# Two norms split by token stream, a dense half computed stream by stream, and a gather placed directly behind the ranks

## The chip, the core and the metric

The kernel runs on one core of a Trainium2 chip. The metric is the time of one execution on the device in microseconds (us). Below, TensorE (PE) is the matrix engine, VectorE (DVE) and ScalarE (ACT) are the two elementwise engines, GpSimd (POOL) a slower one, and SyncE (SP) issues most of the DMAs.

## What is computed

Two layers of a diffusion backbone over 256 latent and 256 context tokens (two streams, two tiles of 128 tokens each) of width 1024, all in float32:

```python
for l in range(DEPTH):                       # DEPTH = 2
    h  = _modulate(x, norm1_w[l], sh1, sc1)  # rms norm * (1 + scale) + shift
    hc = _modulate(ctx, norm1_w[l], csh1, csc1)
    p, pc = h @ w_in[l], hc @ w_in[l]        # last layer: only the key/value columns of pc
    ...                                      # attention, retention, convolution
    x = x + g1 * (concat(att, ret, cnv) @ w_out[l])
    h2 = _modulate(x, norm2_w[l], sh2, sc2)
    x = x + g2 * _channel_mixer(h2, l, ...)
    # the context goes the same way in layer 0 and ends there

def _swiglu(h, wg, wu, wd):                  # layer 0, D_FF = 2816
    return (silu(h @ wg) * (h @ wu)) @ wd

def _moe(h, router, wg, wu, wd):             # layer 1, 8 experts, D_FF_EXPERT = 3584
    top_v, top_i = lax.top_k(h @ router, 2)
    combine = sum(one_hot(top_i) * softmax(top_v)[..., None])
    return sum(combine[..., e:e+1] * _swiglu(h, wg[e], wu[e], wd[e]) for e in range(8))
```

## The kernel before

**Products.** Weights and activations are split into a high part (float32r, written by ScalarE) and a low part (the rest, a subtraction on VectorE). `three` (L517) issues three products for each pair of operands: high x high, high x low, low x high. Weights come as items of up to 1 MB: SyncE loads one into one of four `raw` slots when the item that held the slot has its low part (to L1076), ScalarE writes the high part into a `parts` slot that TensorE has finished with (`split_to`, L1126; `split_expert`, L1234), VectorE the low part (L1457, L1841). The order is fixed for each engine by the program text; semaphores (`after`, `wait_ge`) join them.

**Norms.** ScalarE squares each token tile with a sum (`squares`), GpSimd takes the root (`root_squares`), VectorE scales (`scale_tokens`), TensorE transposes the scaled tiles into banks (`turn_normalized`, L558), VectorE modulates the latent banks and ScalarE the context ones (`modulate`), ScalarE writes high parts into `hTr`, VectorE low parts. In front of the dense layer and of layer 1 this runs for all four tiles together, after the residual of the last of them.

**Order around the change.** Output projection of layer 0 (`project_out`, two halves of 512 columns, tiles in the order 2, 3, 0, 1, where 2 and 3 are the context), second norm, dense layer (`dense_ffn`: 11 tiles of gate and up, two halves of the down product, and once more), first norm of layer 1 for both streams, in-projection of layer 1 (`project_in`, first the query columns, for which only the latent tiles are needed), attention and the rest, output projection, second norm of the latent tiles, `routing`, `place_tokens`, `scatter_matrices`, `spread_gate`, then `experts`. The experts run in four pairs (`pair`, a loop for the last three); each expert has seven slices of gate, up and down. Tokens of an expert are gathered with a product (`gather`, matrix `PA` of zeros and ones), and its output goes back with a product per token tile and half (`scatter`, matrix `SCAT`, in full float32) and an addition into `ACC`. The matrix of the scatter carries the combine weights; it is made by `weighted` on VectorE, turned by `scatter_matrices` on TensorE and kept in `SA`.

**Banks.** VectorE evacuates four banks in turn (`open_v`), ScalarE three (`open_a`). TensorE waits in `open_v` or `open_a` until the bank's last user is read.

## Time and profile before

| | before |
|---|---|
| runs, us | 2016.98, 2017.33, 2013.34; median 2016.98 |
| profiled execution, us | 2017.29, its span 2015.3 |
| busy, share of the span | PE 92%, weight loads 74%, DVE 67%, ACT 51%, POOL 6% |
| chain that ended last | PE 78%, DVE 11%, DMA 5%, ACT 3%, issue 2%, POOL 1% |
| DMA | 472.89 MB, mean 235 GB/s |
| first product of the dense layer | 369.49 us |
| first product of layer 1 | 771.86 us |
| first product of the experts | 994.66 us |

A timeline row gives start, duration, engine, source line, operation, and in brackets how long the engine had been idle and who released it. Where rows of one kind are merged, "x32" counts them and the duration covers them all. Busy time is no measure of how well TensorE is used, since the ends of its products are modelled and overlap; its idle times are.

### The profile page before, as it was taken

The page shows a single profiled execution, that of the slowest core. Times are in us where ns is not written, and L with a number is a line of the kernel's source. Part 1 is how long each engine was busy: PE and PEld are TensorE (multiplying, and loading weights), DVE is VectorE, ACT ScalarE, POOL GpSimd, SP SyncE. Part 2 cuts the span into 40 slices and gives each one's busy share as a digit, 9 for nine tenths or more (in the row PEclk, how much of TensorE's full clock was granted, in tenths as well). Part 3 has the DMA queues.
Part 4 walks back from the last instruction along what each step waited for, and adds up shares of the span by engine and source line. Part 5 has one row for each costly group of instructions (what it writes and reads, how often), then busy time and mean ns, then how long its engine had stood idle before and what let it go on. Part 6 is the DMA issues. An engine that isn't in the chain of part 4 may idle for free.

```text
span 2015.3 us, 23614 instructions
## 1 busy us (share of the span) xinstructions
PE 1857.1 (92%) x8916; PEld 1499.9 (74%) x8916; DVE 1350.3 (67%) x1286; ACT 1036.7 (51%) x972; POOL 115.4 (6%) x127
## 2 busy tenths in 40 slices
PE   4899888799999987998699999999999999999997
PEld 1777457688788767857588888788887888878885
DVE  1464964432243225685698988989888888888886
ACT  2322542432122115263377776777767767667773
POOL 0021710100000000250000000000000000000000
PEclk9899989899999998998799999999999999999999
DMA  8223832432333112392499998999999999899994
GB/s 291 84 88 125 302 133 71 106 88 90 84 105 100 58 58 89 105 334 84 145 370 334 374 366 313 358 336 373 357 328 354 346 357 373 328 350 339 366 367 157
DMA packets 245914, 472.89 MB, mean 235 GB/s; under 512 B 10546, under 2 KB 60564, under 8 KB 245804
## 3 DMA queue, kind: packets, MB, share of 16 engines
q1 hardware_dynamic: 241856, 468.67, 65.5%
q10 hardware_dynamic: 3948, 2.67, 0.5%
q8 instruction: 79, 1.29, 0.3%
q14 instruction: 31, 0.25, 0.0%
HBM read 470.26 MB, written 1.05 MB: 234 GB/s over the span
## 4 chain that ended last, share of the span: by engine, by line
PE 78%; DVE 11%; DMA 5%; ACT 3%; issue 2%; POOL 1%; SPq 0%; ACTq 0%; DVEq 0%; POOLq 0%
PE bank L519 23%; PE bank L521 22%; PE bank L520 22%; DVE parts L1479 2%; DVE parts L1464 2%; PE bank L537 1%; PE bank L920 1%; DMA raw<-in_ada_w_dram 1%; PE bank L934 1%; ACT parts L1240 1%; PE bank L961 1%; DMA raw<-in_moe_w_gate_dram 1%; DMA raw<-in_moe_w_up_dram 1%; PE bank L753 1%; ACT parts L1138 1%
## 5 line engine op out<-in xcount | busy, mean ns | idle before, releaser
L1479 DVE TENSOR_TENSOR parts<-raw,parts 128x2048 fp32r<-128x2048 f32 x336 | 765.0, 2289 | 113.1 <-ACT parts L1240 112.0
L1240 ACT ACTIVATE parts<-raw 128x2048 fp32r<-128x2048 f32 x336 | 642.4, 1918 | 259.6 <-DMA raw<-in_moe_w_up_dram 90.1
L519 PE MATMUL bank<-parts,XEr 128*128 128x512 f32 x896 | 355.0, 396 | 7.7 <-DVE XEr L1479 3.9
L521 PE MATMUL bank<-parts,XEr 128*128 128x512 f32 x896 | 350.0, 391 | 0.0
L520 PE MATMUL bank<-parts,XEr 128*128 128x512 f32 x896 | 349.6, 390 | 0.0
L1138 ACT ACTIVATE parts<-raw 128x2048 fp32r<-128x2048 f32 (+1 forms) x62 | 113.3, 1831 | 331.1 <-PE bank L521 308.4
L1464 DVE TENSOR_TENSOR parts<-raw,parts 128x2048 fp32r<-128x2048 f32 (+1 forms) x62 | 135.4, 2188 | 194.1 <-ACT parts L1138 194.0
L519 PEld LDWEIGHTS bank<-parts,XEr 128*128 128x128 f32 x896 | 168.6, 188 | 43.4 <-DVE parts L1479 5.9
L521 PEld LDWEIGHTS bank<-parts,XEr 128*128 128x128 f32 x896 | 168.6, 188 | 35.8
L520 PEld LDWEIGHTS bank<-parts,XEr 128*128 128x128 f32 x896 | 168.8, 188 | 33.5
L519 PE MATMUL bank<-parts,HTr 128*128 128x512 f32 x448 | 180.8, 404 | 0.7 <-DVE parts L1479 0.7
L521 PE MATMUL bank<-parts,HTr 128*128 128x512 f32 x448 | 174.6, 390 | 0.0
L520 PE MATMUL bank<-parts,HTr 128*128 128x512 f32 x448 | 174.4, 389 | 0.0
L519 PE MATMUL bank<-hTr,parts 128*128 128x512 f32 (+1 forms) x416 | 160.7, 386 | 5.3 <-DVE parts L1464 2.1
L521 PE MATMUL bank<-hTr,parts 128*128 128x512 f32 (+1 forms) x416 | 158.6, 381 | 0.0
L520 PE MATMUL bank<-hTr,parts 128*128 128x512 f32 (+1 forms) x416 | 158.6, 381 | 0.0
L519 PE MATMUL bank<-parts,hTr 128*128 128x512 f32 (+1 forms) x320 | 124.3, 389 | 18.5 <-DVE hTr L1479 8.6
L521 PE MATMUL bank<-parts,hTr 128*128 128x512 f32 (+1 forms) x320 | 122.4, 382 | 0.0
L520 PE MATMUL bank<-parts,hTr 128*128 128x512 f32 (+1 forms) x320 | 122.2, 382 | 0.0
L1479 DVE TENSOR_TENSOR HF<-bank,SG 128x512 f32<-128x512 f32 x22 | 15.2, 692 | 145.4 <-PE bank L521 145.4
L519 PEld LDWEIGHTS bank<-parts,HTr 128*128 128x128 f32 x448 | 84.1, 188 | 22.0 <-issue 3.3
L520 PEld LDWEIGHTS bank<-parts,HTr 128*128 128x128 f32 x448 | 84.2, 188 | 20.3 <-issue 3.3
(220 smaller groups left out, 2319.0 us busy)
## 6 DMA issues: line engine op xcount, KB each, us to landing
raw<-in_moe_w_gate_dram SPq DMA_DIRECT2D x112, 1024.0 KB, 7.0
raw<-in_moe_w_up_dram SPq DMA_DIRECT2D x112, 1024.0 KB, 7.2
raw<-in_moe_w_down_dram SPq DMA_DIRECT2D x112, 1024.0 KB, 6.6
raw<-in_ada_w_dram SPq DMA_DIRECT2D x28, 1024.0 KB, 7.8
more<-in_ada_w_dram SPq DMA_DIRECT2D x20, 1024.0 KB, 7.5
raw<-in_w_in_dram SPq DMA_DIRECT2D x12, 1024.0 KB, 5.4
raw<-in_ffn_w_gate_dram SPq DMA_DIRECT2D x22, 512.0 KB, 4.0
raw<-in_ffn_w_up_dram SPq DMA_DIRECT2D x22, 512.0 KB, 5.3
```

What stands on the lines that cost most here:

```text
L519: nc.tensor.matmul(out, st[0], mv[0], start=start, stop=False)
L520: nc.tensor.matmul(out, st[0], mv[1], start=False, stop=False)
L521: return nc.tensor.matmul(out, st[1], mv[0], start=False, stop=stop)
L537: mm = nc.tensor.matmul(b[32 * j:32 * j + 32, :], cond[:, half * KT // 2 + j, c0:c0 + 32], w[:, j, :], start=opening, stop=closing)
L753: mm = nc.tensor.matmul(OB[:, head * 64:(head + 1) * 64], PT[:, n % 4, kb * P:(kb + 1) * P], proj[:, kb, C_V + 64 * g:C_V + 64 * g + 64], ...
L920: mm = nc.tensor.matmul(M[k // 4][:, (k % 4) * P:(k % 4 + 1) * P], xn[:, t, k * P:(k + 1) * P], PA[:, t, bass.ds(i * 2 + j, 1), :].rearran ...
L934: nc.tensor.matmul(M[h][:, :], SCAT[:, ee % 2, t * P:(t + 1) * P], YS[:, h * 512:(h + 1) * 512], start=True, stop=True).then_inc(scatter_f ...
L961: mm = nc.tensor.transpose(T[g % 2][:, j * P:(j + 1) * P], HE[:, g % 2, j * P:(j + 1) * P], ident)
L1138: nc.scalar.activation(parts[:, s, 0, 0:k * width], raw[:, r, 0:k * width], ACT.Copy).then_inc(hi_ready, 1)
L1240: nc.scalar.activation(parts[:, n % PARTS, 0, :], raw[:, r, :], ACT.Copy).then_inc(hi_ready, 1)
L1464: nc.vector.tensor_tensor(parts[:, s, 1, 0:k * width], raw[:, r, 0:k * width], parts_f[:, s, 0, 0:k * width], ALU.subtract).then_inc(lo_re ...
L1479: return nc.vector.tensor_tensor(out, a, b, op)
```

## The change

1. *Second norm of layer 0.* The context tiles are scaled, transposed, modulated and split first (`modulate_second(1)`), while the last latent tile still gets its residual; then the latent tiles. TensorE's first feed-forward tile (`first_hidden`) is computed per stream, 256 columns at a time, with the latent transposes between the context's gate and up products.
2. *Last half of the last dense down product.* It runs first for the latent tiles over all three items, which stay in their slots, then for the context tiles. The latent norm of layer 1 (`squares(early=True)`, `scale_tokens(early=True)`, `modulate_first`, `first_low`) runs beside the context half, its transposes (`turn_stream(0)`) go ahead of that half's last item. The context norm of layer 1 comes inside the first column slice (`turn_stream(1)`, `modulate_context`). The decay factors move behind it.
3. *Routing.* The matrix `PA` is written directly behind the ranks, and the first gather needs only it. The scatter matrices are the transposed `PA` (`turn_places`, in the first slice of the first pair); the combine weight is multiplied in when the scattered rows are added (`share`). One of four splits and the clearing of `ACC` leave VectorE's way; the spreading of the gate moves into the output projection of layer 1.
4. *Scatter.* The expert's output is split into a high and a low part (`YS`), `SCAT` is float32r, and each product of the scatter becomes two. The gathered tokens' high and low parts are written in halves.

```diff
             def dense_ffn():
+                first_hidden()
 ...
+            def turn_second(s, banks):
+                after(xn_ready, TT)
+                for kp, b in enumerate(banks):
+                    for kk in range(2):
+                        for t in range(TT):
+                            k = 2 * kp + kk
+                            mm = nc.tensor.transpose(b[:, (kk * TT + t) * P:(kk * TT + t + 1) * P],
+                                                     xn[:, s * TT + t, k * P:(k + 1) * P], ident)
+                    mm.then_inc(a_full if kp % 2 else v_full, 1)
+            def first_hidden():
+                turn_second(1, open_second(1))
+                n, hi, lo = next_item()
+                x_banks = open_second(0)
+                outs = [open_a(("gate", 0)), open_v(("up", 0))]
+                for s in (1, 0):
+                    c = slice(s * SEQ, (s + 1) * SEQ)
+                    for half, b in enumerate(outs):
+                        for k in range(KT):
+                            if half == 0 and k % (KT // 2) == 0:
+                                after(h_lo, KT // 4)
+                            mm = three(b[:, c], (hi[:, k, half * P:(half + 1) * P], lo[:, k, half * P:(half + 1) * P]),
+                                       (hTr[:, 0, k, c], hTr[:, 1, k, c]), k == 0, k == KT - 1)
+                        if s == 0:
+                            mm.then_inc(v_full if half else a_full, 1)
+                        elif half == 0:
+                            turn_second(0, x_banks)
 ...
-                    for half in range(2):
+                    for half in range(2 if p0 == 0 else 1):
 ...
+                held = []
+                for s in range(2):
+                    outs = [open_v() for _ in range(TT)]
+                    for j, (f0, f1) in enumerate(ff_split):
+                        if s == 0:
+                            held.append(next_item())
+                        n, hi, lo = held[j]
+                        if s and f1 == HALF_FF:
+                            turn_stream(0)
+                        for f in range(f0, f1):
+                            for t in range(TT):
+                                tok = slice((s * TT + t) * P, (s * TT + t + 1) * P)
+                                mm = three(outs[t][:, :], (HFr[:, 0, f, tok], HFr[:, 1, f, tok]),
+                                           (hi[:, f - f0, :], lo[:, f - f0, :]), f == 0, f == HALF_FF - 1)
 ...                                                       # project_in
-                            after(h_lo, KT // 2)
+                            after(h_lo, KT // 4 if layer else KT // 2)
+                            if layer and t == 1 and a == C_Q and k0:
+                                turn_stream(1)
 ...                                                       # project_out
+                    if layer and half == 0:
+                        spread_gate(5, (0,))
 ...                                                       # TensorE, experts
-                        nc.tensor.matmul(M[h][:, :], SCAT[:, ee % 2, t * P:(t + 1) * P], YS[:, h * 512:(h + 1) * 512],
-                                         start=True, stop=True).then_inc(scatter_full, 1)
+                        for part_ in range(2):
+                            mm = nc.tensor.matmul(M[h][:, :], SCAT[:, ee % 2, t * P:(t + 1) * P],
+                                                  YS[:, part_, h * 512:(h + 1) * 512], start=part_ == 0, stop=part_ == 1)
+                        mm.then_inc(scatter_full, 1)
+                def turn_places():
+                    pe.wait_ge(places, 2 * part + 2)
+                    for q in range(PAIRS):
+                        if q >= 2:
+                            pe.wait_ge(places_read, PAIRS * part + q - 1)
+                        ...                               # four transposes of PA into T[q % 2]
+                        mm.then_inc(places_full, 1)
 ...                                                       # SyncE
                 if n == first["ffn"] + 2:
-                    sp.wait_ge(v_full, job[("mixed", 0)])
+                    sp.wait_ge(act_mix, 1)
 ...                                                       # ScalarE
+                def expert_high(i, ee):
+                    act.wait_ge(down_done, i * PAIR_SLICES + (s0 + EF_SLICES * (ee + 1) + CREDIT))
+                    for h in range(2):
+                        nc.scalar.activation(YS[:, 0, h * 512:(h + 1) * 512], Y[h][:, :], ACT.Copy).then_inc(y_high, 1)
 ...
                 squares(order_of(layer))
                 if layer == 0:
+                    modulate_second(1)
+                    modulate_second(0)
+                    split_to(O + 7)
                     small_loads(1)
-                    modulate(1)
 ...
+                    squares(range(TT), early=True)
+                    split_to(first["in", 1] + 1)
+                    after(mod1_ready)
+                    modulate_first()
+                    split_to(first["in", 1] + 2)
 ...                                                       # VectorE
+                if layer == 0:
+                    for t in (2, 3, 0):
+                        add_gated(1, t, True)
+                    scale_tokens((2, 3))
+                    add_gated(1, 1, True)
+                    modulate_second(1)
+                    dve.wait_ge(x_ready, x_count[0])
+                    scale_tokens((0, 1))
+                    modulate_second(0)
+                    split_to(O + 7)
 ...
+                    scale_tokens(range(TT), early=True)
+                    split_to(first["in", 1] + 1)
+                    first_low()
+                    for t in range(TT, NT):
+                        add_gated(1, t, True)
 ...                                                       # next layer, then the second item's low part
-                scale_tokens(range(NT))
+                scale_tokens(range(TT if layer else 0, NT))
 ...
-            for n in range(PARTS):
+            for n in range(PARTS - 1):
                 split_expert(0, n, 0)
             route()
             place_tokens(0)
-            nc.vector.memset(ACC_t[:, :], 0.0).then_inc(scatter_read, 1)
+            split_expert(0, PARTS - 1, 0)
 ...
-                        tt(acc, M[h][:, :], acc, ALU.add).then_inc(scatter_read, 1)
+                        nc.vector.scalar_tensor_tensor(acc, M[h][:, :], share[:, ee % 2, t:t + 1], acc, ALU.mult, ALU.add)\
+                            .then_inc(scatter_read, 1)
```

## Rows read from the trace of the kernel before

**Rows 1.** The page's first part: busy time of each engine.
```profile
PE 1857.1 (92%) x8916; PEld 1499.9 (74%) x8916; DVE 1350.3 (67%) x1286; ACT 1036.7 (51%) x972; POOL 115.4 (6%) x127
```

**Rows 2.** Timeline of TensorE in front of the dense layer: start, duration, operation.
```profile
362.18 6.17 PE L568 MATMUL bank<-const,xn 128*128 128x128 f32 x32 [15.79 <-DVE xn L1512]
369.49 0.47 PE L519 MATMUL bank<-hTr,parts 128*128 128x512 f32 x1 [1.14 <-DVE hTr L1479]
```

**Rows 3.** Timelines of VectorE and ScalarE in the second norm of layer 0.
```profile
343.71 0.69 DVE L1479 TENSOR_TENSOR YG<-bank,gb 128x512 f32<-128x512 f32 x1 [1.21 <-PE bank L521]
346.43 0.69 DVE L1479 TENSOR_TENSOR YG<-bank,gb 128x512 f32<-128x512 f32 x1 [1.30 <-PE bank L521]
...
357.22 0.75 DVE L1512 TENSOR_SCALAR xn<-X,rstd 128x1024 f32<-128x1024 f32 x1 [0.80 <-POOL rstd L1403]
...
365.04 1.00 DVE L1526 TENSOR_SCALAR hTf<-bank,scl,ada 128x256 f32<-128x256 f32 x2 [0.71 <-PE bank L568]
365.95 1.28 DVE L1479 TENSOR_TENSOR hTr<-hTf,hTr 128x512 fp32r<-128x512 f32 x2
...
354.01 1.04 ACT L1161 ACTIVATE xn<-X 128x1024 f32<-128x1024 f32 x1
...
354.95 0.19 ACT L1161 ACTIVATION_READ_ACCUMULATOR xn<-X 128x1 f32 x1
...
366.14 1.02 ACT L1169 ACTIVATE hTf<-bank,ada,scl 128x256 f32<-128x256 f32 x2
367.04 1.16 ACT L1175 ACTIVATE hTr<-hTf 128x512 fp32r<-128x512 f32 x2
```

**Rows 4.** Timeline of TensorE: last dense half, norm of layer 1, second column slice.
```profile
718.76 0.70 PE L519 MATMUL bank<-parts,HFr 128*128 128x512 f32 x1 [2.93 <-DVE YG L1479]
...
764.54 6.37 PE L568 MATMUL bank<-const,xn 128*128 128x128 f32 x32 [13.98 <-DVE xn L1512]
...
785.58 0.41 PE L519 MATMUL bank<-parts,hTr 128*128 128x384 f32 x1 [2.56 <-DVE parts L1464]
```

**Rows 5.** Busy time by stretch: length, PE, PEld, DVE, ACT, POOL, PEclk, DMA share, GB/s.
```profile
788.00:790.00 2.00, 2.00 (x8) 2.00 (x8) 0.00 (x0) 0.00 (x0) 0.00 (x0) 0.50 1.01 330
```

**Rows 6.** Timelines of TensorE, VectorE and ScalarE between layer 1's projection and the experts.
```profile
954.29 3.63 PE L568 MATMUL bank<-const,xn 128*128 128x128 f32 x16 [4.41 <-DVE xn L1512]
...
986.99 3.81 PE L920 MATMUL bank<-PA,xn 128*128 128x128 f32 x32 [1.38 <-DVE ACC L2004]
994.66 0.50 PE L519 MATMUL bank<-parts,XEr 128*128 128x512 f32 x1 [3.87 <-DVE XEr L1479]
...
959.04 8.89 DVE L1479 TENSOR_TENSOR parts<-raw,parts 128x2048 fp32r<-128x2048 f32 x4
...
974.08 1.95 DVE L1823 TENSOR_SCALAR XF<-const,top 128x128 f32<-128x128 f32 x8
...
992.29 1.06 ACT L1254 ACTIVATE XEr<-XF 128x1024 fp32r<-128x1024 f32 x1 [1.74 <-DVE XF L1853]
```

**Rows 7.** Timeline of TensorE: products of 256 columns following one another.
```profile
837.66 0.28 PE L520 MATMUL bank<-hTr,parts 128*128 128x256 f32 x1
837.78 0.28 PE L521 MATMUL bank<-hTr,parts 128*128 128x256 f32 x1
```

**Rows 8.** Expert stage: a scatter in the chain, two stretches, groups, one load.
```profile
1139.97 1.72 PE bank L934 x4
...
1240.00:1260.00 20.00, 18.73 (x82) 15.00 (x81) 18.06 (x12) 14.66 (x9) 0.00 (x0) 1.00 0.77 281
1640.00:1720.00 80.00, 80.00 (x355) 64.85 (x354) 71.86 (x44) 57.71 (x39) 0.00 (x0) 1.00 1.01 366
...
L1240 ACT ACTIVATE parts<-raw 128x2048 fp32r<-128x2048 f32 x336 | 642.4, 1918 | 259.6 <-DMA raw<-in_moe_w_up_dram 90.1
...
L1542 DVE SCALAR_TENSOR_TENSOR decay<-distance,dneg,decay 128x512 f32<-128x512 f32 x8 | 5.5, 747 | 0.1
...
raw<-in_moe_w_gate_dram SPq DMA_DIRECT2D x112, 1024.0 KB, 7.0
```

291 lines of the change are left out of this document (206 added, 85 removed).

## The prediction

> **What bounds the kernel now.** I read the page first (shares of the span, busy tenths), then TensorE's waits, then each engine's timeline in the three places that the change touches, and last the busy time by stretch of the expert stage. TensorE is busy for 92% of the span [rows 1]: nearly all of what can be won is pauses of TensorE, and there are few. The reader should see three. Between the output projection of layer 0 and the dense layer it waits 15.8 us for the normalized tokens, then transposes for 6.2 us at half clock, and the first product stands at 369.49 [rows 2]; the last one before the pause had ended at 362.18 - 15.79 = 346.4. Between the dense layer and layer 1 it waits 2.9 us for a bank ahead of the last half [rows 4], 14.0 us for the normalized tokens [rows 4] and, after the first column slice, 2.6 us for split weights [rows 4]. Before the experts it works in scraps between 954.29 - 4.41 = 949.9 and 994.66, 45 us, while VectorE ranks tokens and writes matrices [rows 6]. After such pauses come stretches in which the granted clock is 0.50, the 1.2 GHz level: after the wait that ended at 785.58 it stood at 0.50 at 788 to 790 [rows 5]. In the expert stage TensorE has no pause to speak of except at the pair boundaries, where 20 us hold 18.7 us of work and the loads drop to 281 GB/s [rows 8]. So the stage goes by TensorE, with the loads right behind it.
>
> **Second norm of layer 0.** Work on TensorE stays the same: 32 transposes and 48 products of 512 columns, now 96 of 256. A 256-column product follows the last one after 0.12 us [rows 7], a 512-column one after 2.72 / 12 = 0.227 us (one token tile's 12 products separate the two multiplies at 343.71 and 346.43) [rows 3], so halving the width costs 96 x 0.12 - 48 x 0.227, some 0.6 us. The order is 2, 3, 0, 1, so the context tiles 2 and 3 are full at 338.3 and 341.0, and their residual is added by 342.5. ScalarE squares tile 2 from 341.2 and tile 3 until 343.7 (1.04 + 0.19 each), and from the end of a square to the scaled tile it is 357.22 - 355.14 = 2.1 us [rows 3]: context scaled at 347.4. TensorE pauses 1.0 us and transposes. ScalarE squares tile 1 first (until 350.1: its residual comes after the scaling), then takes 1.02 us for a bank and 0.58 for a high part, VectorE 0.99 and 0.64 [rows 3]: four high parts are out at 354.5, the low parts of the first half at 353.1. TensorE starts the gate product of the context at 353.4, needs 2.8 us for it, waits until 356.7 for the latent tiles, transposes them (3.1 us at half clock), and does the remaining three quarter-items in 8.5 us: first feed-forward tile done at 368.3. Before, that tile ends at 369.49 + 0.5 + 10.9 = 380.9. **-12.5 us** (-9 to -15: the hops of semaphores are in the rows, but a pause of 2.8 us in the middle can bring a half-clock stretch of 1.9 us). Its cover: the latent norm lies under the up product of the context; were that gone, 5 us would return. Of the queues: the load of the third feed-forward item now waits for the last SiLU of the mixing instead of the end of the projection; it goes out earlier, and nothing behind it on the queue is due sooner. The small loads of ScalarE's queue come behind the norm instead of in front of it.
>
> **Last dense half by streams, joined to layer 1.** The half opened four banks, so it waited for all four evacuations, 2.9 us, and its first nine products ran at half clock (0.43 us apart, 1.8 us lost) [rows 4]. By streams it opens two, free 2.7 us sooner: start at 716.1, and I take the half-clock stretch as gone too. Latent tiles are then full at 716.1 + 66 x 0.227 = 731.1, and 15 us of context products lie over their residual (2.7), squares, scaling (to 736.8). The transposes come after two of the three items at 742.0, about 2.1 us at full clock, and the down product ends at 748.2. ScalarE modulates beside it (four times 1.02 + 0.58 and a hop, until 749.2), so the first slice starts at 748.2 without a wait, first half to 753.6. The second item's slot frees at 748.2: its high part is out at 751.1, but on VectorE the low part is queued behind the context's residual (752.6), squares (753.8) and scaling (755.6): ready at 757.9. That is the wait that the change adds, 4.3 us, behind it the whole in-projection. Then 2.7 + 2.1 (context transposes) + 2.7 us: the slice of 384 columns begins at 765.2. With 1 us for hops and clock, 766; before it is 785.58 [rows 4]. **-19.5 us** (-14 to -22). Next late is the context's low part, due at 769.3, ready at about 768: an even race, up to 2 us.
>
> **Ranks and first gather.** Removed ahead of the first gather: one of four splits (8.89 / 4 = 2.2 us), the memset, the weighted matrices, their transposes and copies; the first write of a matrix stands at 974.08, the gather at 986.99 [rows 6]. The gate's spreading (16 products, by the gather's row 16 x 0.12 = 1.9 us) moves into the output projection of layer 1, where TensorE is full: +1.9 us. So: the first write at 974.08 - 0.2 (a small memset in front of it) - 2.2 + 1.9 + 0.2 (room for a hop) = 973.8; the first expert's two writes at 0.24 us each (1.95 / 8) [rows 6], gather from 974.4. TensorE stood idle before, so I take half clock, 7.0 us where the row has 3.81: 981.5. VectorE is through its 16 writes and the split at 980.3; last half of the gathered tokens 1.4 us, low part of the first half 0.7: experts start at 983.8 instead of 994.66, -10.9 us. But 16 transposes come into the first pair. They are some 2 us of TensorE; the third of them waits for ScalarE's copy of the first, and that is queued behind a split of 1.92 us [rows 8]: 3.8 us. **-7 us** (-3 to -10).
>
> **Scatter.** Before, one tile of one expert is four full-precision records in 1.72 us [rows 8]; after, four products of the width and type of the gate products, 4 x 0.227 = 0.91 us. 16 such, two of them in the tail, where ScalarE's copy ahead of VectorE's subtraction takes half back: 14 x 0.81 + 0.7 = 12 us. Of it the six at the start of pairs two to four fall where the supply has just dropped [rows 8], and I count half: **-9.5 us** (-3 to -13). On VectorE the copy becomes a subtraction of the same length; the add becomes an operation with a scalar, 747 ns where the nearest row has it [rows 8] against 0.69, +2 us in 1000, under TensorE's work. ScalarE gets 1.2 us more per expert. **Gathered high part in halves**: a half (0.53 of 1.06 us [rows 6]) goes ahead of the wait for VectorE, three boundaries: **-1 us** (0 to -1.5).
>
> A rule against this term: the rows show 366 GB/s over 80 us with DMA share 1.01 [rows 8]. The Trainium skill, SBUF — State Buffer, section A bandwidth-pool intuition that's wrong, gives about 358 GB/s between HBM and one core and calls HBM nearly always the end-to-end bottleneck. The trace does not agree with the figure: measured stretches pass it. By it the 352 MB of expert weights take at least 984 us (an estimate from that page), the scatter would still gain, but with little room left; by the trace's rate the room is larger.
>
> The memset of the accumulator goes to GpSimd beside VectorE's splits. The same page, section SBUF: two separate sides, says that the two engines share a port pair under an exclusive lock, but a VectorE operation with two SBUF inputs only against a GpSimd one that reads SBUF. A memset reads nothing, so by this rule it is free; no row here shows the pair together.
>
> **Sum.** -12.5 - 19.5 - 7 - 9.5 - 1 = -49.5 us against the profiled execution's own 2017.3 (span 2015.3 and 2.0 around it), which is 0.3 above the median of the runs: 1967.8, say **1968 us**.
>
> **Rivals.**
> *The supply takes over in the expert stage.* For it: share of DMA at 1.0 and 366 GB/s in the full stretches; where TensorE has only products it asks for 1.05 MB per 2.8 us, 374 GB/s. Against: per pair TensorE has extra work of gathers and scatters worth over 10 us that the loads don't need, and the boundary costs them about 20 x (1 - 281/366) = 4.6. Then -9.5 and -1 go: 1978.5. Chance 0.15.
> *New short pauses bring half clock.* Each of three joints (after the context's transposes, after the first slice's half, after the gather) costs 1.9 us more and the last dense half keeps its own 1.8: 1975.5. For it: rows 5 after a wait of 2.6 us. Against: after 16 us of pause the feed-forward started with 0.227 us products, since transposes went before. 0.15.
> *The joint doesn't join.* In-order queues put the other stream's work ahead, so that both norms end as late as before: only -7, -9.5 and -1 stay: 2000. Against: the orders above, worked through engine by engine. 0.05.
> *The added wait on ScalarE starves the ring; slower than before.* ScalarE now waits for an expert's last down product in front of its next splits. If at every of the eight expert ends the four raw slots drain, one load of 7.0 us [rows 8] is lost each: 8 x 7 = 56, so 2024. It decides from 49.5 / 8 = 6.2 us per expert end. Against: in the middle of a pair the split in front of the wait has waited for the same down product already, to free its slot; at the pair boundary VectorE waits for it now in the same place. 0.03.
>
> **How the numbers follow.** Forecast 0.62. Ends of the five terms together give 1956 and 1988; not all fall to one side, so 1956 to 1984, which takes in the first two rivals and leaves out the last two and a tail. About 0.2% is what a measurement of this kernel can tell from no change, 4 us: faster 0.95, same 0.02, slower 0.03.
>
> **What would show it.** TensorE's wait for xn in front of the transposes: 1 us in the first joint, none in the second; the last dense half starting under 1 us after the half before; a wait for split weights of 4 us in the first slice of layer 1; experts starting 43 us (12.5 + 19.5 + 10.9) earlier than now, at about 952; a scatter of 0.91 us; from there to the end about 7 us less than the 1020 of now. Wrong it would be with waits of TensorE for parts in each pair (supply), clock 0.50 in stretches that now have 1.00, or a wait for xn over 5 us.

## The result: 2.7% faster, and where the 54 us lie

The changed kernel takes 1961.78 us (median of four executions, 1959.30 to 1965.86) against 2017.15 of the kernel before: a ratio of 0.9731 with a 95% interval of 0.9711 to 0.9751. The forecast was 1968 within 1956 to 1984. The profiled execution of the changed kernel took 1963.41 us, with a span of 1961.6.

The page of the changed kernel, first part and chain of work that ended last:

```profile
PE 1836.7 (94%) x8964; PEld 1494.4 (76%) x8964; DVE 1346.2 (69%) x1282; ACT 1048.7 (53%) x1001; POOL 113.6 (6%) x126
...
PE 63%; DVE 15%; DMA 12%; ACT 5%; issue 4%; POOL 0%; SPq 0%; DVEq 0%; ACTq 0%; POOLq 0%
```

Of the 53.7 us between the spans, 20 are busy time of TensorE (rows 1 against this page) and 33 its pauses. The last chain has changed: before, it was 78% TensorE and 5% DMA; now it runs over transfers and splits for longer stretches. That comes back in the experiments.

Four moments cut the span into sections that can be compared between all kernels, whatever happened ahead of them: the end of the output projection of layer 0 (start of its last product plus 0.39), VectorE's first write of HF (the first feed-forward tile is through), the first product of 384 columns in layer 1, and the first product of the experts. All from the timelines, in us:

| kernel | projection 0 ends | first HF | 384 columns | experts | span | to HF | to 384 | to experts | stage |
|---|---|---|---|---|---|---|---|---|---|
| before | 346.39 | 381.45 | 785.58 | 994.66 | 2015.3 | 35.06 | 404.13 | 209.08 | 1020.6 |
| after | 344.75 | 366.46 | 752.59 | 947.21 | 1961.6 | 21.71 | 386.13 | 194.62 | 1014.4 |
| difference | -1.64 | | | | -53.7 | -13.35 | -18.00 | -14.46 | -6.2 |

**First joint.** The changed TensorE in front of the dense layer, then VectorE and GpSimd in the same stretch:

```profile
344.96 1.94 PE L882 MATMUL bank<-const,xn 128*128 128x128 f32 x16 [0.21 <-DVE xn L1672]
350.60 0.36 PE L530 MATMUL bank<-hTr,parts 128*128 128x256 f32 x1 [3.70 <-ACT hTf L1291]
...
354.65 0.41 PE L532 MATMUL bank<-hTr,parts 128*128 128x256 f32 x1
354.87 2.17 PE L882 MATMUL bank<-const,xn 128*128 128x128 f32 x16
```

```profile
343.40 1.41 DVE L1672 TENSOR_SCALAR xn<-X,rstd 128x1024 f32<-128x1024 f32 x2
344.79 0.69 DVE L1638 TENSOR_TENSOR YG<-bank,gb 128x512 f32<-128x512 f32 x1
...
342.13 0.19 POOL L1554 TENSOR_SCALAR lnt<-ssq 128x2 f32<-128x2 f32 x1 [61.90 <-ACT xn L1244]
342.47 0.70 POOL L1555 TENSOR_TENSOR rstd<-lnt,nhalf 128x2 f32<-128x2 f32 x1
```

Where 15.79 us of waiting stood [rows 2], there are now 0.21 and 3.70. Both context tiles are scaled before the last tile's residual, and the latent transposes at 354.87 wait for nothing. The products of 256 columns just ahead of them follow one another after 0.21 us where full clock has 0.12: behind the wait of 3.70, from 352.0 to 354.8, the granted clock was 0.50, the 1.2 GHz level.

**Second joint.** TensorE from the last dense half on, and the busy time of two stretches:

```profile
700.48 0.47 PE L530 MATMUL bank<-parts,HFr 128*128 128x512 f32 x1
...
726.44 1.47 PE L598 MATMUL bank<-const,xnx 128*128 128x128 f32 x12
...
732.81 0.39 PE L530 MATMUL bank<-parts,hTr 128*128 128x512 f32 x1
...
742.95 0.80 PE L530 MATMUL bank<-parts,hTr 128*128 128x512 f32 x1 [4.54 <-DVE parts L1623]
...
748.10 1.91 PE L598 MATMUL bank<-const,xn 128*128 128x128 f32 x16
...
752.59 0.33 PE L530 MATMUL bank<-parts,hTr 128*128 128x384 f32 x1
```

```profile
742.95:747.95 5.00, 5.00 (x12) 0.50 0.76 230
...
700.00:735.00 35.00, 34.58 (x160) 1.00 0.25 83
```

The waits of 2.93 and 13.98 us [rows 4] are gone, and the first slice starts at 732.81 without one. In their place stands one wait of 4.54 for the split weights, and behind it twelve products at a granted clock of 0.50.

**Third joint.** VectorE, GpSimd and TensorE ahead of the experts:

```profile
931.60 1.80 POOL L1605 MEMSET ACC<- 128x2048 f32 x1 [12.88 <-PE bank L966]
...
931.99 0.17 DVE L1638 TENSOR_TENSOR top<-top,best 128x16 f32<-128x16 f32 x1
932.19 1.24 DVE L1995 TENSOR_SCALAR top<-top 128x16 f32<-128x16 f32 x1
...
934.71 0.17 DVE L1995 TENSOR_SCALAR top<-top 128x16 f32<-128x16 f32 x1
...
938.59 4.18 DVE L2027 TENSOR_SCALAR PA<-const,top 128x128 f32<-128x128 f32 x16
...
939.44 5.26 PE L991 MATMUL bank<-PA,xn 128*128 128x128 f32 x32 [1.31 <-DVE PA L2027]
947.21 0.47 PE L530 MATMUL bank<-parts,XEr 128*128 128x512 f32 x1 [2.51 <-DVE XEr L1638]
```

The gather follows VectorE's first write after 0.85 us; before, 12.9 us lay between them [rows 6]. The odd row is L1995: one operation of 16 columns takes 1.24 us, its twin 2.5 us later 0.17.

**Expert stage.** The scatter in the chain and its group:

```profile
1112.35 0.93 PE bank L1006 x4
```

```profile
L1006 PE MATMUL bank<-YS,SCAT 128*128 128x512 f32 x64 | 19.2, 424 | 2.1 <-DVE YS L1638 2.1
```

Four records in 0.93 us where they took 1.72 [rows 8].

### The profile page after: what moved, and what is told of

Its sections match the earlier page's. It is cut to its first block, busy times and chain, and to the rows that moved or that the text cites. A ratio compares the mean times of both kernels' runs of the same rounds, so it can differ in the third digit from the quotient of the medians.

```text
span 1961.6 us, 23758 instructions
## 1 busy us (share of the span) xinstructions
PE 1836.7 (94%) x8964; PEld 1494.4 (76%) x8964; DVE 1346.2 (69%) x1282; ACT 1048.7 (53%) x1001; POOL 113.6 (6%) x126
## 4 chain that ended last, share of the span: by engine, by line
PE 63%; DVE 15%; DMA 12%; ACT 5%; issue 4%; POOL 0%; SPq 0%; DVEq 0%; ACTq 0%; POOLq 0%
PE bank L530 18%; PE bank L532 18%; PE bank L531 18%; DVE parts L1638 5%; DMA raw<-in_moe_w_gate_dram 5%; ACT parts L1358 3%; DMA raw<-in_moe_w_up_dram 3%; DMA raw<-in_moe_w_down_dram 3%; DMA raw<-in_ada_w_dram 2%; DVE parts L1623 2%; PE bank L548 1%; PE bank L991 1%; DVE gb L1897 1%; PE bank L781 1%; PE bank L1046 1%
## 5 line engine op out<-in xcount | busy, mean ns | idle before, releaser
L530 PE MATMUL bank<-parts,HTr 128*128 128x512 f32 x448 | 175.3, 391 | 1.1 <-DVE HTr L1638 0.7
L531 PE MATMUL bank<-parts,HTr 128*128 128x512 f32 x448 | 174.5, 390 | 0.0
L532 PE MATMUL bank<-parts,HTr 128*128 128x512 f32 x448 | 174.4, 389 | 0.0
L530 PE MATMUL bank<-hTr,parts 128*128 128x512 f32 (+1 forms) x432 | 164.6, 381 | 7.3 <-ACT hTf L1291 3.7
L532 PE MATMUL bank<-hTr,parts 128*128 128x512 f32 (+1 forms) x432 | 162.5, 376 | 0.0
L531 PE MATMUL bank<-hTr,parts 128*128 128x512 f32 (+1 forms) x432 | 162.4, 376 | 0.0
L530 PEld LDWEIGHTS bank<-hTr,parts 128*128 128x128 f32 x432 | 82.2, 190 | 24.0 <-issue 7.2
L530 PEld LDWEIGHTS bank<-parts,HTr 128*128 128x128 f32 x448 | 84.1, 188 | 20.5 <-DVE parts L1638 2.3
```

The costliest lines, as they stand in the source:

```text
L530: nc.tensor.matmul(out, st[0], mv[0], start=start, stop=False)
L531: nc.tensor.matmul(out, st[0], mv[1], start=False, stop=False)
L532: return nc.tensor.matmul(out, st[1], mv[0], start=False, stop=stop)
```

## The experiments

Each ran beside the kernel before; "beside it" is a kernel on the same chip in the same series (e_same with the next three, e_norm2_old to e_four_banks, e_same_2 with the last three). The middle series has no unedited kernel in it, so its medians are compared with unedited kernels of other series, and its sections count for more. The sections of all of them, in us, read as in the table above:

| kernel | median | ratio to before, 95% | to HF | to 384 | to experts | stage |
|---|---|---|---|---|---|---|
| e_same | 1964.88 | 0.9722-0.9753 | 21.72 | 386.14 | 194.69 | 1024.1 |
| e_scatter_fp32 | 1973.49 | 0.9759-0.9795 | 21.69 | 386.13 | 194.66 | 1022.3 |
| e_scatter_one | 1963.89 | 0.9720-0.9754 | 21.69 | 386.13 | 194.68 | 1012.2 |
| e_memset_twice | 1966.26 | 0.9722-0.9762 | 21.73 | 386.16 | 196.12 | 1013.9 |
| e_norm2_old | 1975.93 | 0.9784-0.9824 | 31.55 | 386.66 | 193.61 | 1018.3 |
| e_dense_old | 1981.73 | 0.9820-0.9859 | 21.71 | 403.70 | 194.27 | 1013.8 |
| e_split_early | 1958.39 | 0.9701-0.9739 | 21.71 | 381.96 | 194.23 | 1017.4 |
| e_four_banks | 1963.31 | 0.9727-0.9762 | 21.71 | 386.13 | 196.03 | 1015.5 |
| e_same_2 | 1964.15 | 0.9742-0.9782 | 21.72 | 386.18 | 194.63 | 1014.5 |
| e_less_bytes | 1957.25 | 0.9707-0.9746 | 21.72 | 386.18 | 194.66 | 1008.0 |
| e_less_bytes_one | 1953.44 | 0.9681-0.9718 | 21.73 | 386.16 | 194.63 | 1003.7 |
| e_combined | 1958.87 | 0.9712-0.9747 | 21.71 | 381.97 | 194.45 | 1015.0 |

The table can be read before any single run. The columns "to HF" and "to 384" repeat to 0.05 us wherever their code is the same, so a change of 1 us there is certain. One value seems to break this: "to 384" is 386.66 in e_norm2_old, with the code of the changed kernel from HF on. The moment "first HF" is VectorE's: in the changed kernel it comes 0.8 us after TensorE has finished that tile (365.68), because VectorE still splits weights, and in e_norm2_old 0.03 us after it. So "to HF" shows some 0.5 us less than the new order gains, and "to 384" as much more; the same explains the last 0.4 us between 404.13 and e_dense_old's 403.70.

The stage doesn't repeat: the unedited kernel gave 1014.4, 1024.1 and 1014.5. In that stage one pair of profiles proves nothing under 10 us, and the medians have to speak. They too are blunt: the five executions of one kernel spread over 4 to 9 us, and a difference of two means of five is known to about 3 to 5 us (95% interval).

### The unedited kernel again

> The changed kernel itself, unedited, as the yardstick for the kernels beside it. Both theories: within 0.2% of 1961.8 us. Of the 53.7 us between the two spans, 1.6 us lie before the first edited instruction (the output projection of layer 0 ended at 344.75 us of its execution in the changed kernel's profile against 346.39 before). If they are a matter of the one execution (how long the granted clock stays at half in the first 345 us), the end of that projection lies here somewhere between 344.5 and 346.5; if something in the changed code brings them, it is 344.7 again.

The projection of layer 0 ended at 343.84, and at 347.27 in the highest of the twelve further executions, all with the same code up to there. The 1.6 us ahead of the change are a matter of the execution.

The profiled execution is also the slowest of its five (1972.40), by the stage alone: 1024.1. TensorE's waits in it, whole tail of the kernel, then those of the first profile of the same code:

```profile
PE bank L530 <- DVE parts L1638: 8.3, 15, 0.9
...
PE bank L530 <- DVE HTr L1638: 1.2, 4, 0.5
```

```profile
PE bank L530 <- DVE parts L1638: 4.3, 8, 0.9
...
PE bank L530 <- DVE HTr L1638: 0.7, 1, 0.7
```

Weights came late fifteen times instead of eight. The chain of that execution is 50% TensorE and 19% DMA, against 63 and 12. The same program asks for the same bytes; in the third quarter of the stage they came at 348 GB/s in this execution and at 356 in the first.

### Is the expert stage still TensorE's?

Full-precision scatter, and a scatter with half its products:

```
-                        for part_ in range(2):
-                            mm = nc.tensor.matmul(M[h][:, :], SCAT[:, ee % 2, t * P:(t + 1) * P],
-                                                  YS[:, part_, h * 512:(h + 1) * 512], start=part_ == 0, stop=part_ == 1)
+                        mm = nc.tensor.matmul(M[h][:, :], SCAT[:, ee % 2, t * P:(t + 1) * P],
+                                              YS[:, 0, h * 512:(h + 1) * 512], start=True, stop=True)
```

For the first of them YS and SCAT are F32 as well, so one full-precision product does what two did. The second leaves the low part of the expert outputs out.

> Expert outputs and scatter matrices as float32 and one full-precision product per half instead of two float32r products; ScalarE's copy and VectorE's subtraction stay, so only TensorE changes: 16 tile-experts at 1.72 instead of 0.91 us, +13 us of TensorE. The output keeps full precision. TensorE sets the pace of the expert stage: +9.5 to +13 us (1971 to 1975). The supply of weights sets it: the added work lies in waits for parts, which shrink by as much, under +3 us.

Measured +8.6 us beside e_same (1973.49 - 1964.88), for some 13 us of TensorE; by the means it is 6.4, give or take 4.7 (95%, here and below). The chain is 80% TensorE and 4% DMA again.

> Only the product with the high part of the expert outputs is left in each scatter (the low part is still formed but not multiplied, so the output lacks it): 16 x 0.45 = 7.3 us less on TensorE. TensorE sets the pace: -6 to -7 us (1955). The supply sets it by now: TensorE waits for parts for those 7 us, 0 to -1 us. Between them, with the six scatters at the pair starts lost and the rest won: -4 us.

Measured -1.0 us (1963.89 - 1964.88; by the means -2.0, give or take 4.6), for 7.3 us of TensorE. Two stretches of 50 us of this kernel (length, PE, PEld, DVE, ACT, POOL, PEclk, DMA share, GB/s) show TensorE busy for 47 and 48 of 50 us and the DMA queues almost full; its waits for weights are these:

```profile
1198.52:1248.52 50.00, 47.20 (x209) 37.75 (x208) 45.02 (x31) 35.88 (x25) 0.00 (x0) 1.00 0.96 336
1848.52:1898.52 50.00, 48.19 (x215) 39.23 (x216) 43.72 (x26) 35.81 (x24) 0.00 (x0) 1.00 0.99 352
```

```profile
PE bank L530 <- DVE parts L1637: 6.5, 8, 1.1
```

They are 2.2 us more than in two unedited profiles (4.3 and 4.2) and less than in the third (8.3), so they do not show where the 7.3 us went. By the medians, a microsecond of TensorE costs about 0.66 us above the changed kernel and 0.14 below it; given the spread, that bend is suggested and not shown. If it is there, the supply of weights would explain it, and the next two runs test that by taking bytes away instead of work: they load only 768 of the 1024 columns of each down weight, and the last quarter holds old data, so the result is another.

```
-                            dst = raw[:, n % RAW, :].rearrange("p (k n) -> p k n", k=2)
+                            dst = raw[:, n % RAW, :].rearrange("p (k n) -> p k n", k=2)[:, :, 0:768]
+                            rows = rows[:, :, 0:768]
```

> The loads of the experts' down weights fetch 768 of 1024 columns, 8% fewer bytes in the expert stage, with everything else unchanged (the last quarter of those columns is stale, so the output is another). The supply sets the pace at the margin, as the run with one scatter product suggested: the waits for weights (4 to 8 us) go and the stage becomes as long as TensorE's own work, -5 to -10 us, 1954 to 1958, and its length varies less from execution to execution. TensorE sets the pace and the run with one product had some other loss: -1 to -2 us.

Measured -6.9 us beside e_same_2 (1957.25 - 1964.15), though no instruction of TensorE, ScalarE or VectorE changed. By the means it is 7.2, give or take 3.8: clear of the spread, and the one run that shows the supply costing time in the changed kernel. The stage took 1008.0, the DMA rate fell to 316 GB/s over 1000 us from 346, and the waits for weights from 4.2 to 2.6:

```profile
947.55:1947.55 1000.00, 989.13 (x4592) 819.84 (x4592) 867.61 (x558) 719.54 (x513) 0.00 (x0) 1.00 0.90 316
```

```profile
PE 83%; DVE 9%; DMA 3%; ACT 3%; issue 2%; POOL 0%; SPq 0%; ACTq 0%; DVEq 0%; POOLq 0%
```

> Both at once: 768 of 1024 columns of the down weights are loaded, and only the high part of the expert outputs is multiplied in the scatter (both change the output). If the supply hid the 7.3 us of TensorE's work that the single product saves, they appear now: 7 us less than with fewer bytes alone. If they stay hidden (under 2 us less), something other than the supply holds the stage, such as VectorE's own chain at the scatters.

Measured -3.8 us beside e_less_bytes (by the means -5.1, give or take 3.4). So TensorE's time counts as well when there are fewer bytes. Whether it counts for more than with all bytes, which is what "the supply hid it" claims, these runs don't decide: -1.0 and -3.8 lie within each other's spread. They point that way, no more. The expected 7 did not come; the chain still has 7% DMA, and TensorE waits for weights for 4.1 us, so the supply may not be quite out of the way. Fewer bytes still weren't tried.

> The changed kernel unedited once more, beside the three others on the same chip: their yardstick. Within 0.2% of 1963 us; its expert stage, from the first product to the end, 1014 to 1024 us long (the two profiled executions so far gave 1014.4 and 1024.1, with 4.3 and 8.3 us of waits for weights).

Measured 1964.15 with a stage of 1014.5, as expected.

### The first joint undone

On each engine the norm's order is that of the kernel before. The core of the edit, on TensorE and VectorE (ScalarE and GpSimd alike: `modulate(1)` behind the small loads, one square root per tile):

```
-                first_hidden()
+                turn_normalized((0, 1))
...
-                    for t in (2, 3, 0):
-                        add_gated(1, t, True)
-                    scale_tokens((2, 3))
-                    add_gated(1, 1, True)
-                    modulate_second(1)
-                    dve.wait_ge(x_ready, x_count[0])
-                    scale_tokens((0, 1))
-                    modulate_second(0)
-                    split_to(O + 7)
+                    for t in order_of(layer):
+                        add_gated(1, t, True)
+                    split_to(O + 7)
+                    dve.wait_ge(x_ready, x_count[0])
+                    scale_tokens(order_of(layer))
+                    modulate(1, (0, 1))
```

> The changed kernel with its second norm of layer 0 as before the change: all four token tiles normalized, 32 transposes, then 48 products of 512 columns. My term for this part was 12.5 us (9 to 15), the traces side by side give 13.7 (first feed-forward tile done 15.3 us earlier, less 1.6 that were there before the first edit). If the parts add up: 1961.8 + 13.7 = 1975. If the time was won elsewhere and this joint gives less because the pause with its half-clock transposes only moves: under +9, below 1971.

The median is 14.2 us above the 1961.78 of the changed kernel and 11.1 above e_same, both from other series; in its own place the edit costs 31.55 - 21.71 = 9.84 us, 10.4 up to the 384 columns. The traces side by side gave 13.35, and the sections say why: this kernel has the norm as before and still is 3.5 us quicker in it than the kernel before, 31.55 against 35.06. VectorE of this run ahead of its first scaled tile:

```profile
347.91 4.49 DVE L1620 TENSOR_TENSOR parts<-raw,parts 128x2048 fp32r<-128x2048 f32 x2 [0.58 <-ACT parts L1222]
353.20 0.75 DVE L1669 TENSOR_SCALAR xn<-X,rstd 128x1024 f32<-128x1024 f32 x1 [0.80 <-POOL rstd L1555]
```

The two splits of feed-forward weights stand back to back. In the kernel before, VectorE waited 3.41 us for the second of them, since its load had been held back to the end of the projection; the earlier release (`sp.wait_ge(act_mix, 1)`) stays in this run. The row of the kernel before:

```profile
354.13 2.29 DVE L1464 TENSOR_TENSOR parts<-raw,parts 128x2048 fp32r<-128x2048 f32 x1 [3.41 <-ACT parts L1138]
```
So with the old order the earlier load is worth 3.5 us, and the new order then 9.8. That does not make the load a part of the gain. The changed kernel reaches this item only behind its norm; ScalarE's high part of it, in the kernel before and in the changed one:

```profile
352.19 1.91 ACT L1138 ACTIVATE parts<-raw 128x2048 fp32r<-128x2048 f32 x1 [3.79 <-DMA raw<-in_ffn_w_up_dram]
...
361.90 1.91 ACT L1220 ACTIVATE parts<-raw 128x2048 fp32r<-128x2048 f32 x1
```

Even a load as late as the old one would be there some 11 us before it is needed (361.90 - 352.19, and the 1.6 us that the changed kernel is ahead at this point). Either edit alone removes the 3.41 us: the order by moving the split out of the way, the load by feeding it in time. Undoing one while the other stays puts its price too low. No run held back the load alone, so this rests on the two traces. (The stage of 1018.3 lies within that stage's spread.)

A second piece of the old wait is in rows 3, as the 0.80 us for which the first scaling waited for GpSimd. GpSimd takes the root between a square and its scaling; in the kernel before:

```profile
355.23 1.25 POOL L1402 TENSOR_SCALAR lnt<-ssq 128x1 f32<-128x1 f32 x1 [73.39 <-ACT xn L1161]
```

The same operation takes 0.19 elsewhere, and this one ends (356.48) with VectorE's split (356.42). In e_norm2_old it takes 1.65 and ends at 352.45, the split at 352.40. So from the end of a square to the scaled tile it is 2.1 us in rows 3, but 1.35 in the changed kernel (342.05 to 343.40), where no split runs beside it.

### The second joint undone, and made better

The last dense half goes over four tiles again, and the whole first norm of layer 1 stands behind it, on all four engines:

```
-                    for half in range(2 if p0 == 0 else 1):
+                    for half in range(2):
...
+                else:
+                    turn_normalized((0, 1))
                 project_in(layer)
```

> The changed kernel with the last dense half by four token tiles and the first norm of layer 1 behind it, as before the change. My term was 19.5 us (14 to 22); the traces give 17.7 up to the start of the slice of 384 columns (33.0 less 15.3), and some 2 us more behind it, since the half-clock stretch after the wait of 2.6 us is gone. If the parts add up: 1961.8 + 19.5 = 1981. If the added wait for split weights had eaten more of the gain than I counted: under +14, below 1976.

The median is 1981.73, 17 to 20 us above the unedited medians, the section 403.70 - 386.13 = 17.6 us. The parts add up to within 0.4 us of the traces' 18.0; the 2 us that I expected behind the slice aren't there (194.27 against 194.62).

A side result: this kernel waits 2.56 us for split weights in the place where the kernel before did, and its granted clock stayed at 1.00 behind it.

```profile
770.70 0.41 PE L530 MATMUL bank<-parts,hTr 128*128 128x384 f32 x1 [2.56 <-DVE parts L1589]
...
770.70:774.70 4.00, 4.00 (x23) 1.00 0.74 209
```

In rows 4 and 5 the same wait is followed by 0.50.

```
                     for t in range(TT, NT):
                         add_gated(1, t, True)
+                    split_to(first["in", 1] + 2)
                     dve.wait_ge(x_ready, x_count[0])
```

> VectorE forms the low part of layer 1's second weight item right behind the residual of the context tiles instead of behind their scaling. The high part is out at 735.35, the residual ends at 736.9, so the low part is there at 739.3 instead of 742.9, while TensorE is free at 738.4. My theory of the added wait (low part queued behind the context's norm on VectorE): the wait falls from 4.5 to about 1 us, -3.5 us, and with it the 12 products at half clock behind it, another -2.4: 1956. Rival: the context's scaling, now 2 us later, or its transposes become late, and the time is given back one slice on: 0 to -1 us. Rival on the clock: the wait shrinks but the half-clock stretch stays: -3.5 us.

The section to 384 columns went from 386.13 to 381.96: -4.2 us, certain. TensorE of this kernel:

```profile
739.93 0.50 PE L530 MATMUL bank<-parts,hTr 128*128 128x512 f32 x1 [0.77 <-DVE parts L1623]
743.63 1.53 PE L598 MATMUL bank<-const,xn 128*128 128x128 f32 x12 [0.69 <-DVE xn L1672]
745.89 0.66 PE L598 MATMUL bank<-const,xn 128*128 128x128 f32 x4 [0.73 <-DVE proj L1641]
749.15 0.33 PE L530 MATMUL bank<-parts,hTr 128*128 128x384 f32 x1
```

Wait and half-clock stretch are gone, as my theory had it: -3.8 us for the wait (0.77 instead of 4.54), and the twelve products take 3.0 us (739.93 to 743.63, less the 0.69) instead of 5.15 (742.95 to 748.10), -2.1. The rival took 1.7 back: the context's scaling is now late by 0.69, and the transposes with the rest of the slice take 1.0 longer, with a wait of 0.73 for a bank. The median of 1958.39 goes the same way; its interval overlaps that of the unedited kernels, so the section carries the verdict.

### The third joint

No run puts the old order of ranks, matrices and gather back, so the price of this joint (12.7 us, below) rests on the traces of before and after; the two runs here test parts of it.

Four banks for the place matrices:

```
                     for q in range(PAIRS):
-                        if q >= 2:
-                            pe.wait_ge(places_read, PAIRS * part + q - 1)
                         for e in range(2):
                             for t in range(TT):
-                                mm = nc.tensor.transpose(T[q % 2][:, (e * TT + t) * P:(e * TT + t + 1) * P], PA[:, t, 2 * q + e, :], ident)
+                                mm = nc.tensor.transpose((T + Y)[q][:, (e * TT + t) * P:(e * TT + t + 1) * P], PA[:, t, 2 * q + e, :], ident)
```

> The 16 transposes of the place matrices go into four PSUM banks instead of two, so none of them waits for ScalarE's copy of the first pair, which is queued behind a split of 1.9 us. My theory of their price (3.6 us between the gate product before and the product after, of which 1.7 is that wait): -1.7 us. Rival (the ring of loads runs full in that time anyway, so the wait is only moved to a wait for parts): 0.

```profile
961.39 1.91 PE L1015 MATMUL bank<-const,PA 128*128 128x128 f32 x16
963.06 0.48 PE L530 MATMUL bank<-parts,XEr 128*128 128x512 f32 x1
```

The transposes cost 1.67 us, from 961.39 to the next product at 963.06, instead of 3.61 (958.18 to 961.79): -1.9 in their place. The time (1963.31) shows nothing of it, and can't: this kernel's gather ran 6.74 us instead of 5.26 and the first expert's products behind it partly at half clock (granted clock 0.83 over 10 us from 948.5, where the unedited kernel has 1.00), and the stage's spread is larger than the gain.

A second memset, behind the first:

```
+            step(nc.gpsimd.memset(ACC_t[:, :], 0.0))
             nc.gpsimd.memset(ACC_t[:, :], 0.0).then_inc(scatter_read, 1)
```

> GpSimd clears the accumulator twice, one after the other, 3.6 us instead of 1.8. In the changed kernel's profile one VectorE operation of 16 columns (the first tensor_scalar of the ranks) took 1.24 us where all its like take 0.17, and ended 0.03 us after the memset. If the memset holds VectorE off the port that it needs, the operation lasts until the second memset's end, about 3.1 us, and the experts start 1.8 us later than in the unedited kernel. If the 1.24 us is something else (a first read after the wait), it stays 1.24 and the experts start as before, since nothing else waits for the memset until the first gather.

GpSimd and VectorE, with two memsets:

```profile
934.21 1.80 POOL L1605 MEMSET ACC<- 128x2048 f32 x1 [12.88 <-PE bank L966]
...
934.80 1.24 DVE L1996 TENSOR_SCALAR top<-top 128x16 f32<-128x16 f32 x1
936.07 1.80 POOL L1606 MEMSET ACC<- 128x2048 f32 x1
...
936.49 0.17 DVE L1639 TENSOR_TENSOR top<-const,best 128x16 f32<-128x16 f32 x1
...
937.32 0.58 DVE L1996 TENSOR_SCALAR top<-top 128x16 f32<-128x16 f32 x1
937.94 0.18 DVE L1639 TENSOR_TENSOR top<-top,const 128x16 f32<-128x16 f32 x1
```

Neither number came as written. The first operation still took 1.24 us, but it ends with the first memset, and its twin, which takes 0.17 without a memset beside it, is now held 0.58 until the second one ends. So the memset does hold VectorE, one instruction at a time: VectorE slips in between the two. The additions and reductions in between took 0.17 to 0.18 beside either memset. Cost: 1.07 us for one, 0.41 more for the second; the rest of the 1.5 us in this run's third section is its gather (6.66 us instead of 5.26, with 0.36 less waiting behind it). The 1.07 is not a constant: in e_split_early the same operation took 0.76.

The Trainium skill has this: SBUF — State Buffer, section SBUF: two separate sides, lets a VectorE operation in a two-port mode block against GpSimd's whole instruction, and the Trainium skill, VectorE: DVE Perf Modes, section What auto-detection actually checks, gives that mode to an operation with a single source and its destination in SBUF, under conditions on their outer dimensions. L1995 has one source, a tensor_tensor has two. The trace agrees, with 1.24 us beside 0.17. One source alone doesn't decide, though: the tensor_reduce beside the memset has one as well and took 0.17.

### All three together

```
-            pool.wait_ge(v_full, job["routed"])
-            nc.gpsimd.memset(ACC_t[:, :], 0.0).then_inc(scatter_read, 1)
...
                 step(tt(comb, comb, tmp, ALU.add))
+                nc.vector.memset(ACC_t[:, 0:D_MODEL], 0.0).then_inc(scatter_read, 1)
                 b = take()
...
                 gathered(0, 0)
+                if part == 0:
+                    nc.vector.memset(ACC_t[:, D_MODEL:TT * D_MODEL], 0.0)
```

with the edits of e_split_early and e_four_banks.

> The low part of the second weight item of layer 1 ahead of the context's scaling (-4.2 us at the slice of 384 columns by its own run), four banks for the place matrices (-1.7), and the accumulator cleared by VectorE, half of it in VectorE's wait of 1.0 us for the counts and half behind the first gathered tokens, so that no memset of GpSimd holds VectorE (-1.1). Sum -7 us: the experts start 5.3 us earlier, the span is 7 shorter, 1956. Rival: the expert stage is held by the supply, and the 1.7 us inside it go into a wait for weights: -5.3.

```profile
929.73 0.17 DVE L1991 TENSOR_SCALAR top<-top 128x16 f32<-128x16 f32 x1
...
934.00 0.91 DVE L2008 MEMSET ACC<- 128x1024 f32 x1 [0.28 <-DVE top L1634]
```

The held operation is back at 0.17, and half the memset fits into VectorE's wait: from the first ranking operation to the first matrix write it is 6.0 us instead of 7.0. The experts start at 943.88, 3.3 us ahead of the unedited kernel's first profile, though the projection ended 1.0 later. The second joint gives 4.2 of it again; of the 1.07 of the memset only 0.2 reaches the third section (194.45 against 194.62), since the ranking started 0.7 later behind the 384 columns and the gather took 5.77. So the sections up to the experts give 4.3 us, not the 5.3 expected. The time is 5.3 us under e_same_2 beside it (1958.87 against 1964.15): the rival's number, but by the means it is 6.0, give or take 3.2, so it tells neither from the 7 expected nor whether the gain inside the expert stage was lost. The intervals against the kernel before, 0.9712 to 0.9747 and 0.9742 to 0.9782, barely touch.

## Why the prediction was right, step by step

Forecast -49.5, measured -53.9 by the profiled executions. Of the measured, 1.6 us ahead of the change and some 3.6 that go with the granted clock (third joint, below) are no part of the forecast's mechanism; without them it is 48.7. That the sum came as close as it did is in part luck: with e_same's expert stage (1024.1) in place of the first profile's, the last row below would read +3.5. Section by section:

| section | predicted | measured | what the difference is |
|---|---|---|---|
| ahead of the change | 0 | -1.6 | the execution (343.84 to 347.27 with the same code) |
| second norm of layer 0 | -12.5 | -13.35 | pause 0.21 instead of 1.0, transposes at full clock |
| dense half and norm of layer 1 | -19.5 | -18.0 | half clock behind the added wait |
| from there to the experts | -10.9 | -14.5 | granted clock, in stretches away from the joint |
| expert stage | -6.6 | -6.2 | one pair of profiles; see below |

**First joint.** Right in order and size; one reading was off. I worked out a new state (368.3) and didn't ask what the old one's 15.79 us consisted of: 3.41 of them were VectorE's wait for split weights in front of the scaling, and 0.80 its wait for GpSimd's root, late beside a split. The second went into the forecast: the 2.1 us from a square to its scaled tile took 1.35, and the context was scaled at 344.8 instead of 347.4 (1.6 of the difference lie ahead of the change). The earlier load, booked at nothing, is worth 3.5 us with the old order (e_norm2_old) and by the traces nothing with the new one, so that booking stands. The half-clock stretch that I allowed for came (0.21 us spacing up to 354.87), and the latent transposes, for which I had 3.1 us and a wait until 356.7, took 1.9 without one.

**Second joint.** The order held point by point: context half under the latent norm, no wait for xn, down product 32.3 us long (predicted 32.1), first slice without a wait, 4.54 us for the second item's split (predicted 4.3). The step that was mis-sized is the 384-column slice: 19.8 us behind the first instead of 17.8. I priced the added wait at its own length and not at the stretch behind it; the twelve products at clock 0.50 cost 2.1 us more than at full clock in e_split_early, which wins most of both back. The last dense half started 0.5 us after the start of the last product before it (699.97), as predicted under 1 us.

**Third joint.** Here two numbers have to be held apart. From the first transposes of layer 1's second norm to the experts I had 12.8 us less (10.9, and the 1.9 of gate spreading that leaves), and it is 40.37 - 27.65 = 12.7. But inside, nothing fits so well: the gather took 5.26 us instead of 7.0, the routing products 6.97 instead of 5.24 at half clock, and the memset that I called free held VectorE 1.07. That error was one of reading: the rule on two inputs covers the splits, but the memset ran beside the ranking, and the half of the rule on the two-port mode I left out. From the 384 columns to that point I had +1.9 for the spreading, and it is -1.7. Over the twelve stretches of 14 us that follow the slice's start, the granted clock falls short of full by 0.85 stretches in sum in the profile of before and by 0.55 in that of after, 4.2 us of clock. Part of it is the half-clock stretch behind the wait of 2.56 [rows 4, 5], which e_dense_old doesn't have with the same wait, so the second joint alone doesn't bring the difference. Nor does it look like spread between executions: all thirteen profiles of the changed kernel and its variants fall short by 0.52 to 0.57, ten of them stretch for stretch to within 0.01. Whether the kernel before always has 0.85, or its one profile was an odd one, stays open. The transposes of the place matrices cost 3.6 (predicted 3.8).

**Expert stage.** The predicted 0.91 us for a scatter is 0.93. The term of 9.5 us is 8.6 by e_scatter_fp32's median, within its range, as is the 6.4 of the means. The single pair of profiles (-6.2) would have looked like a hit for any term between 0 and 15, since the stage of one program varies by 10 us. And the sentence "the stage goes by TensorE, with the loads right behind it" is too simple for the changed kernel: e_scatter_fp32 shows that TensorE's time costs, e_less_bytes that bytes cost too. The kernel before wasn't tested for this. Its chain (78% TensorE, 5% DMA) and that of the changed kernel (63% and 12%) suggest that the change used up the distance. The rival that the supply takes over, to which I gave 0.15, came true in part at most: 8.6 of 13 us came through at the scatters, and 1.0 of the 7.3 of the next step (e_scatter_one), if one takes the medians at their word. The sum for that rival was also too kind to the supply: at 0.227 us a product, the twelve products of an item take 2.72 us and not 2.8, and ask for 385 GB/s, more than the 366 of rows 8.

**The other rivals.** The joints join (e_norm2_old, e_dense_old); ScalarE's wait in front of its splits starves nothing, since the unedited stage isn't longer. New half-clock stretches came behind both waits of over 3 us: thirteen 256-column products 0.1 us longer each, 1.3 us, and the 2.1 us in layer 1. Against them the one at the start of the last dense half is gone, so of that rival's 7.5 us only a part came.

## What to carry to other kernels

Read what a long wait consists of on every engine in front of it, not only on the one that ends it. Where two edits each remove the same piece of it, undoing one of them alone does not show what that piece was worth. Price a new wait of TensorE with the half-clock stretch behind it, here a third to a half of the wait again. And where a stage has TensorE at 99% and the DMA queues at 95%, try removing bytes as well as work, with enough executions to tell a few us apart: one profile doesn't say which of the two the next change must go for, and five executions each barely did.

## What the runs showed of the hardware

- A split on VectorE (tensor_tensor, two inputs in SBUF) ran beside a GpSimd tensor_scalar of one column that took 1.25 and 1.65 us instead of 0.19, and ended with the split both times.
- A memset of GpSimd held a VectorE tensor_scalar of 16 columns for 1.24 us instead of 0.17, until the memset's end; tensor_tensor and tensor_reduce beside it took 0.17. Between two memsets VectorE got through.
- The same loads come at different speeds from execution to execution: with the same program the expert stage took 1014.4, 1024.1 and 1014.5 us, and TensorE waited for weights 4.3, 8.3 and 4.2 us in them. The recorded waits hold about half of the 10 us; where TensorE's other half went, the profile doesn't show.
- Whether a short wait is followed by half clock isn't fixed by its length: 2.56 us of waiting in the same place led to 0.50 in the kernel before and to 1.00 in e_dense_old, and a gather of 32 products behind a wait of 1.3 us took 5.2 to 6.7 us in thirteen profiles (5.26 in the changed kernel's, 6.74 in that of e_four_banks, which has the same code up to there).
